# Moving the second root of a norm ahead of the residual at the seam of a two-block kernel

## The reference

```python
def first_block(...):
    ...
    h = h + rmsnorm(m @ w_out[l], norm_mix_post[l])
    u2 = rmsnorm(h, norm_mlp_pre[l])
    a = jnp.square(jax.nn.relu(u2 @ w_up[l]))
    h = h + rmsnorm(a @ w_down[l], norm_mlp_post[l])
def second_block(...):
    shift, scale, gate = adaln(c, w_ada_mix[i], b_ada_mix[i])
    h = rms_norm(x, norm_mix_w[i]) * (1.0 + scale) + shift
    proj = h @ w_in
    ...
```

## Time and profile before

| | |
|---|---|
| median of 3 runs | 1815.55 us (1814.15 to 1815.65) |
| profiled execution, its own time | 1813.71 us |
| its span | 1812.0 us |
| TensorE matmul busy | 1736.1 us, 96% |
| VectorE, ScalarE, GpSimd busy | 884.9, 689.5, 824.9 us |
| last down tile read, first product of the second block | 741.82, 770.32 us |

### The profile page before, as it was taken

The page is one execution under the profiler, slowest core; times in us unless marked ns, Lnnn a source line. Parts: engine busy times, 40 slices in busy tenths (PEclk is TensorE's granted clock), DMA queues, the critical chain, the costliest instruction groups (busy, mean ns, idle before and its releaser), DMA issues. The chain is left out here.

```text
span 1812.0 us, 22090 instructions
## 1 busy us (share of the span) xinstructions
PE 1736.1 (96%) x7978; PEld 1399.6 (77%) x7978; DVE 884.9 (49%) x1246; ACT 689.5 (38%) x934; POOL 824.9 (46%) x610
## 2 busy tenths in 40 slices
PE   7999999889999999599999999999999999999997
PEld 5777776768888888478887878777888788888886
DVE  3343356373444445469888887874515411101112
ACT  4333254422222222246547464665523323222231
POOL 4333434544464646434343434425346344664453
PEclk9999999999999999799999999999999899999998
DMA  4121112335353534223323223212222222332232
GB/s 175 70 70 69 69 70 73 113 130 183 126 199 119 196 118 158 70 78 99 128 93 116 93 93 116 93 70 71 92 93 93 93 93 93 116 139 93 93 116 93
DMA packets 30198, 193.25 MB, mean 107 GB/s; under 512 B 3360, under 2 KB 3360, under 8 KB 11328
## 3 DMA queue, kind: packets, MB, share of 16 engines
q1 hardware_dynamic: 23184, 158.89, 24.6%
q10 hardware_dynamic: 6960, 33.62, 5.5%
HBM read 190.34 MB, written 2.16 MB: 106 GB/s over the span
## 5 line engine op out<-in xcount | busy, mean ns | idle before, releaser
L405 POOL TENSOR_TENSOR w_lo<-w_raw,w_hi 128x512 fp32r<-128x512 f32 x588 | 804.6, 1400 | 960.3 <-ACT w_hi L913 960.3
L430 PE MATMUL gemm_bank<-a_hi,w_hi 128*128 128x512 f32 x1224 | 487.9, 399 | 0.3 <-ACT w_hi L913 0.3
L431 PE MATMUL gemm_bank<-a_lo,w_hi 128*128 128x512 f32 x1224 | 478.6, 391 | 0.0
L913 ACT ACTIVATE w_hi<-w_raw 128x2048 fp32r<-128x2048 f32 x147 | 280.3, 1907 | 220.5 <-PE gemm_bank L437 173.3
L437 PE MATMUL gemm_bank<-a_hi,w_lo 128*128 128x512 f32 x1224 | 308.9, 395 | 4.4 <-POOL w_lo L405 4.4
L430 PEld LDWEIGHTS gemm_bank<-a_hi,w_hi 128*128 128x128 f32 x1224 | 230.8, 189 | 55.2 <-issue 7.8
L437 PEld LDWEIGHTS gemm_bank<-a_hi,w_lo 128*128 128x128 f32 x1224 | 229.0, 189 | 56.1 <-POOL w_lo L405 6.1
L431 PEld LDWEIGHTS gemm_bank<-a_lo,w_hi 128*128 128x128 f32 x1224 | 230.8, 189 | 48.2 <-issue 1.9
L1623 DVE SCALAR_TENSOR_TENSOR aux_bank<-scratch,gcol,aux_bank 128x511 f32<-128x511 f32 (+15 forms) x240 | 165.7, 733 | 15.0 <-ACT aux_bank L1105 12.7
L468 PE MATMUL gemm_bank<-a_hi,w_hi 128*128 128x512 f32 x352 | 130.3, 415 | 25.3 <-ACT a_hi L923 17.6
L430 PE MATMUL gemm_bank<-b_hi,w_hi 128*128 128x512 f32 x368 | 148.7, 404 | 0.0
(11 more groups left out here) (274 smaller groups left out, 2072.4 us busy)
## 6 DMA issues: line engine op xcount, KB each, us to landing
w_raw<-weights_dram SPq DMA_DIRECT2D x147, 1024.0 KB, 4.7
arena<-ada_dram ACTq DMA_DIRECT2D x32, 768.0 KB, 4.3
acc<-cum_rows ACTq DMA_DIRECT2D x8, 512.0 KB, 3.8
h<-x_t_dram SPq DMA_DIRECT2D x4, 512.0 KB, 7.4
row_b<-cum_rows ACTq DMA_DIRECT2D x4, 512.0 KB, 4.8
scratch<-cum_rows ACTq DMA_DIRECT2D x4, 512.0 KB, 4.3
out_t_dram<-arena SPq DMA_DIRECT2D x8, 256.0 KB, 2.2
cols<-cols_dram SPq DMA_DIRECT2D x1, 279.0 KB, 2.8
```

What stands on the lines that cost most here:

```text
L405: ins = pool.tensor_tensor(wlo[s][:, w], raw[s][:, w], whi[s][:, w].bitcast(F32), ALU.subtract)
L430: pe.matmul(gemm_bank[bank][:, :], whi[slot][:, w], hi[:, k, :], start=(n == 0), stop=False)
L431: pe.matmul(gemm_bank[bank][:, :], whi[slot][:, w], lo[:, k, :], start=False, stop=False)
L913: act.activation(whi[panel % 2][:, :], raw[panel % 2][:, :], ACT.Copy).then_inc(w_hi_ready, 1)
```

## The change

The root of the second block's norm is no longer taken from squares of the new `h`. With r the inverse root of the MLP's norm, the sum of squares of h + r (gain y) is r squared times the sum of (gain y) squared, plus 2 r times the sum of gain y h, plus the sum of h squared. The last is kept from the earlier norm (`h_sum`); the other two are added up beside the last down tiles (`gained_sum`, `cross_sum`), on ScalarE and VectorE. TensorE sums the three behind the last tile, the last chunk apart. VectorE puts them together in five 128x4 steps (`new_sum`). The second inverse has a buffer and a bank of its own (`rinv2`, `aux[2]`). VectorE makes the added parts in three buffers, GpSimd adds them to `h`, VectorE multiplies the operand. The first product of the second block starts three tiles together (T_DT and both of panel 57), where there were two and one. The residual behind the mixer passes its product through PSUM banks instead of `tmp`. Panel 26 is rounded ahead of the MLP's relus. The small gains `gain2` are made beside chunk 6 of the last down tiles.

```diff
+cross = acc31[:, 1, :]
+cross_sum = row_b[:, 1, :]
+gained_sq = [tmp[:, 0, :], tmp[:, 1, :]]
+gained_sum = acc31[:, 0, :]
+step3 = [tmp[:, 0, :], tmp[:, 1, :], acc31[:, 0, :]]
...
+panels_of(0, P_MLP // 2 + 1)
+add_squares(pool, 1)
+panels_of(P_MLP // 2 + 1, P_DT // 2 + 1)
+for k in range(KC):
+    pool.wait_ge(post_step, KC + k + 1)
+    pool.tensor_tensor(h[:, k, :], h[:, k, :], step3[k % 3], ALU.add).then_inc(h_ready, 1)
+panels_of(P_DT // 2 + 1, P_END // 2)
...
+def sums_of_parts():
+    pe.wait_ge(sq_sum_step, 17)
+    pe.wait_ge(gained_step, KC - 2)
+    pe.wait_ge(cross_step, 2 * (KC - 2) + 1)
+    for n, of in ((0, sq_sum), (1, gained_sum), (2, cross_sum)):
+        for j in range(QT):
+            mm = pe.matmul(aux[0][:, 3 * j + n:3 * j + n + 1], of[:, j * P:(j + 1) * P], ones[:, 0:1],
+                           start=(n == 0 and j == 0), stop=False, skip_group_check=True)
+    mm.then_inc(early_sums, 1)
+def sums_of_last():
+    pe.wait_ge(cross_step, 2 * (KC - 2) + 2)
+    for j in range(QT):
+        pe.matmul(aux[0][:, 3 * j + 2:3 * j + 3], cross[:, j * P:(j + 1) * P], ones[:, 0:1],
+                  start=False, stop=False, skip_group_check=True)
+    pe.wait_ge(ysq_ready, 16)
+    for j in range(QT):
+        mm = pe.matmul(aux[0][:, 3 * j:3 * j + 2], sq[:, 1, j * P:(j + 1) * P], one_gain2[:, :],
+                       start=False, stop=(j == QT - 1), skip_group_check=True)
+    mm.then_inc(sum_done, 2)
 mlp(0, True)
 with pe.Fori(1, MLP_GROUPS) as i:
     mlp(i, False)
-sums_of_sum(17, 16)
+sums_of_parts()
+sums_of_last()
 spread(3)
-sums(2)
-spread(4)
-tile_pair([(0, P_DT, T_DT, 0, 0, wide(0)), (0, P_GRP, T_GRP, 0, 0, wide(0))], a_hi, a_lo,
-          (a_hi_ready, 3 * KC + 1), (a_lo_ready, 3 * KC + 1), True)
+pe.wait_ge(rinv_ready, 5)
+for j in range(QT):
+    mm = pe.matmul(aux[2][:, j * P:(j + 1) * P], rinv2[:, j:j + 1].to_broadcast([P, P]), ident[:, :],
+                   start=True, stop=True)
+mm.then_inc(r_ready, 1)
+def first_three():
+    three = [(P_DT, T_DT, 0), (P_GRP, T_GRP, 0), (P_GRP, T_GRP + 1, 1)]
+    for k in range(KC):
+        pe.wait_ge(a_hi_ready, 3 * KC + k + 1)
+        for panel, t, j in three:
+            w = slice((2 * k + j) * P, (2 * k + j + 1) * P)
+            if k == 0:
+                pe.wait_ge(w_hi_ready, panel + 1)
+                pe.wait_ge(bank_free[t % 4], t // 4 + 1)
+            pe.matmul(gemm_bank[t % 4][:, :], whi[panel % 2][:, w], a_hi[:, k, :], start=(k == 0), stop=False)
+            if k == 0:
+                pe.wait_ge(w_lo_ready, panel + 1)
+            pe.matmul(gemm_bank[t % 4][:, :], wlo[panel % 2][:, w], a_hi[:, k, :], start=False, stop=False)
+    for k in range(KC):
+        pe.wait_ge(a_lo_ready, 3 * KC + k + 1)
+        for panel, t, j in three:
+            w = slice((2 * k + j) * P, (2 * k + j + 1) * P)
+            mm = pe.matmul(gemm_bank[t % 4][:, :], whi[panel % 2][:, w], a_lo[:, k, :],
+                           start=False, stop=(k == KC - 1))
+            if k == KC - 1:
+                mm.then_inc(tile_done, 1)
+first_three()
...
-g(1)
...
+round_weights(0, P_MLP + 2, 0, T_MLP + 2, 0)
...
-if j % 2 == 1:
+if j % 2 == 1 and not (first and j == 1):
...
+if j < KC - 1:
+    if j >= 3:
+        act.wait_ge(gained_step, j - 2)
+    act.activation(gained_sq[j % 2] if j else gained_sum, y[:, j, :], ACT.Square,
+                   scale=col("norm_mlp_post", j)).then_inc(sq_ready, 1)
...
-roots(3, sum_done, 4)
-squares(2)
-roots(4, sum_done, 5)
+mlp(0, True, False)
+with act.Fori(1, MLP_GROUPS - 1) as i:
+    mlp(i, False, False)
+mlp(MLP_GROUPS - 1, False, True)
+act.wait_ge(sum_done, 4)
+act.activation(root[:, :], aux[0][:, 0:3 * QT].rearrange("p (j n) -> p j n", n=3)[:, :, 0], ACT.Sqrt,
+               bias=eps[:, 0:1], scale=1.0 / D).then_inc(root_ready, 1)
+act.wait_ge(new_step, 5)
+act.activation(root[:, :], new_sum[:, :], ACT.Sqrt, bias=eps[:, 0:1], scale=1.0 / D).then_inc(root_ready, 1)
...
+if n == 2:
+    dve.tensor_copy(h_sum[:, :], aux[0][:, 0:QT])
...
-    dve.scalar_tensor_tensor(tmp[:, k % 2, :], y[:, k, :], col(gain, k), aux[1][:, :],
+    dve.scalar_tensor_tensor(aux[2 + k % 2][:, :], y[:, k, :], col(gain, k), aux[1][:, :],
                              ALU.mult, ALU.mult).then_inc(post_step, 1)
 if k >= 1:
     dve.wait_ge(post_step, base + k)
-    dve.tensor_tensor(h[:, k - 1, :], h[:, k - 1, :], tmp[:, (k - 1) % 2, :], ALU.add) \
+    dve.tensor_tensor(h[:, k - 1, :], h[:, k - 1, :], aux[2 + (k - 1) % 2][:, :], ALU.add) \
...
+if last:
+    if j >= 2:
+        dve.wait_ge(cross_step, 2 * j - 1)
+    if j == KC - 1:
+        dve.wait_ge(early_sums, 1)
+    dve.scalar_tensor_tensor(cross if j else cross_sum, y[:, j, :], col("norm_mlp_post", j), h[:, j, :],
+                             ALU.mult, ALU.mult).then_inc(cross_step, 1)
 if last and j < 7:
+    if j:
+        dve.wait_ge(cross_step, 2 * j)
+        dve.tensor_tensor(cross_sum, cross_sum, cross, ALU.add).then_inc(cross_step, 1)
     dve.wait_ge(ysq_ready, 8 + j + 1)
     dve.wait_ge(sq_sum_step, 10 + j)
     dve.tensor_tensor(sq_sum, sq_sum, sq[:, j % 2, :], ALU.add).then_inc(sq_sum_step, 1)
+    if j:
+        dve.wait_ge(sq_ready, 2 * KC + j + 1)
+        if j >= 2:
+            dve.wait_ge(gained_step, j - 1)
+        dve.tensor_tensor(gained_sum, gained_sum, gained_sq[j % 2], ALU.add).then_inc(gained_step, 1)
+if last and j == KC - 2:
+    dve.wait_ge(mod_ready, MLP_GROUPS)
+    for part, name in enumerate(("norm_mix_w", "norm_ffn_w")):
+        dve.scalar_tensor_tensor(gain2[:, KC * part:KC * part + KC],
+                                 mod[:, 24 * part + KC:24 * part + 2 * KC], 1.0,
+                                 cols[:, COLS[name]:COLS[name] + KC], ALU.add, ALU.mult) \
+            .then_inc(gain2_ready, 1)
...
-residual(3, "norm_mlp_post", 8, 24)
-dve.wait_ge(mod_ready, MLP_GROUPS)
-for part, name in enumerate(("norm_mix_w", "norm_ffn_w")):
-    dve.scalar_tensor_tensor(gain2[:, KC * part:KC * part + KC], mod[:, 24 * part + KC:24 * part + 2 * KC], 1.0,
-                             cols[:, COLS[name]:COLS[name] + KC], ALU.add, ALU.mult).then_inc(gain2_ready, 1)
+def summed(n):
+    return aux[0][:, 0:3 * QT].rearrange("p (j n) -> p j n", n=3)[:, :, n]
+def added_part(k):
+    if k >= 3:
+        dve.wait_ge(h_ready, KC + k - 2)
+    dve.scalar_tensor_tensor(step3[k % 3], y[:, k, :], col("norm_mlp_post", k), aux[1][:, :],
+                             ALU.mult, ALU.mult).then_inc(post_step, 1)
+def new_operand(k):
+    dve.wait_ge(h_ready, KC + k + 1)
+    dve.scalar_tensor_tensor(a_raw[:, k, :], h[:, k, :], gain2[:, k:k + 1], aux[2][:, :],
+                             ALU.mult, ALU.mult).then_inc(pre_raw, 1)
+inverse(3)
+dve.wait_ge(rinv_ready, 4)
+dve.tensor_tensor(new_sum[:, :], summed(1), rinv[:, :], ALU.mult).then_inc(new_step, 1)
+dve.wait_ge(new_step, 1)
+dve.scalar_tensor_tensor(new_sum[:, :], summed(2), 2.0, new_sum[:, :], ALU.mult, ALU.add).then_inc(new_step, 1)
+dve.wait_ge(new_step, 2)
+dve.tensor_tensor(new_sum[:, :], new_sum[:, :], rinv[:, :], ALU.mult).then_inc(new_step, 1)
+dve.wait_ge(new_step, 3)
+dve.tensor_tensor(new_sum[:, :], new_sum[:, :], h_sum[:, :], ALU.add).then_inc(new_step, 1)
+dve.wait_ge(new_step, 4)
+dve.tensor_scalar(new_sum[:, :], new_sum[:, :], 0.0, None, ALU.max).then_inc(new_step, 1)
+dve.wait_ge(r_ready, 4)
+added_part(0)
+inverse(4)
+added_part(1)
+added_part(2)
 dve.wait_ge(gain2_ready, 2)
-dve.wait_ge(h_ready, 2 * KC)
-normed_shifted(4, 2, 3 * KC, 0)
+dve.wait_ge(r_ready, 5)
+for k in range(KC):
+    new_operand(k)
+    if k + 3 < KC:
+        added_part(k + 3)
+for k in range(KC):
+    dve.wait_ge(a_hi_ready, 3 * KC + k + 1)
+    dve.scalar_tensor_tensor(a_lo[:, k, :], a_raw[:, k, :], mod[:, k:k + 1], a_hi[:, k, :].bitcast(F32),
+                             ALU.add, ALU.subtract).then_inc(a_lo_ready, 1)
```

27 lines of the change are left out of this document (15 added, 12 removed).

## The result

The changed kernel took 1800.56 us (median of 4 runs, 1798.72 to 1800.85), the kernel before beside it 1815.6 (1814.15 to 1817.13): ratio 0.9911, 95% interval 0.9897 to 0.9925. So 15.0 us faster; the two profiled executions differ by 12.9 in their spans (1812.0 and 1799.1). The forecast was 11.2 faster, 1804.4, with a range of 1798 to 1809.5.

What follows compares the result with a forecast made beforehand. TensorE, busy 96% of 1812.0 us, was taken as the bound, so time is won where it idles or runs slowly. Head -2.7 and junction -8.5 make -11.2: 1804.4 us against the median 1815.55, range 1798 to 1809.5.

Steps and rivals of the forecast that it cites:

- The seam, to the first product: Between the blocks, last projection read to next block's first product: first product at 757.1, 13.2 earlier; gap 28.5 to 15.
- The small steps: Five 128x4 VectorE steps between the two roots, some held by GpSimd: 3.0 taken, 1.0 with none waiting, 5.0 with three.
- The outer bounds 754.4 and 759.9: Next block's first product, in the old trace's clock: 754.4 with no waits in the steps, 759.9 with all.
- GpSimd's addition: Residual add to h between the blocks: 1.53 a chunk, the median of 1.29 to 1.77 for GpSimd's two-operand steps.
- the rival of the GpSimd pace: First three tiles: GpSimd's adds take 2.3 a chunk, the operand comes 5 later, 1809 in all; chance 0.07.
- Given back: Behind the first three tiles: ScalarE's chain up to the sigmoid loses its cover; 4.7 us lost, junction -13.2 + 4.7 = -8.5.
- The head of the MLP: First block, residual through PSUM and panel 26 rounded early: stage -2.7, from -0.7 to -5.5.
- 2.0, 1.75 and 0.7: VectorE's gains in the MLP's head: residual, step no longer meeting GpSimd, waiting gone; together 4.5.
- The residual through PSUM: First block's adds to h: 0.38 less each, eight times 3.0; 2.0 taken, between 0 and 3.0.
- The rule weighed: Skill's rule: two-SBUF-input VectorE and SBUF-reading GpSimd instructions exclude each other; all SBUF-only small steps could be held, 2.0 later.
- the first rival: MLP wait really goes or small steps aren't held: clock stays up, junction starts near 755; 1800 to 1802, chance 0.17.
- the signs listed ahead: Gap of 15, small steps over 0.8, adds 1.3 to 1.8, sigmoid 5 behind tiles, panel 58 idling, `b_hi` wait 3 to 4.

Runs made afterwards that it cites:

- e4: The changed kernel without VectorE's wait for `early_sums` before the last cross product; 1799.22 us.
- e11: e8 with the results of the second to fifth of VectorE's five small steps in PSUM instead of SBUF; 1794.75 us.
- e5: The changed kernel with both edits at the MLP's head undone: residual product in SBUF, panel 26 rounded at its old place; 1809.42 us.
- a0: The changed kernel again, unedited, as the base of the follow-up set; 1801.66 us.
- e2: The changed kernel with panel 26 rounded at its old place, behind the second relu; 1802.82 us.
- e7: The changed kernel with the decay's exp moved to the program's start, so no Exp table is loaded behind the first tiles; 1800.78 us.
- e3: The changed kernel with two tiles together at the seam and the third behind them, as before the change; 1796.06 us.
- e1: The changed kernel with the first block's residual product back in an SBUF tile; 1802.66 us.
- e8: The changed kernel with two tiles at the seam, the third behind, and VectorE's wait for the early sums left out; 1794.35 us.
- e9: e8 with 1, 2 and 4 thrown-away 128x512 products in TensorE's three waits at the seam; 1793.50 us.

## Why the prediction held, point by point

**The seam, to the first product: right, 14.3 for 15.3.** The mechanism held, but the number is in part luck, since steps missed in both directions. The last chunk and the sums were let wait 1.2: the early sums follow TensorE's last product after 0.28, so nothing was late. But the eight last matmuls, put at 2.3, took 3.2, and that used the gain up: the first reciprocal ended 7.5 behind the last read, exactly as foreseen. The last product behind the `early_sums` wait was there as written (2.28 idle on VectorE, 0.93 on TensorE). The small steps were put at 3.0 between 1.0 and 5.0; they took 1.4 (745.17 to 746.59), with one held for 0.62. From the same order they took 1.0 to 2.0 in the other kernels; in e4, with two held for 1.2 each, they took 3.0, and in e11, with none held, 1.0. The 5.0 was never reached. That left 1.6 too much in the sum, of which 0.8 went to a wait that it did not have: at the low clock the first spread lasts until 747.28, and the first added part, with the second reciprocal behind it, waits for that (0.72). The outer bounds 754.4 and 759.9 are given without their full working; the small steps alone make 2.0 of it each way. GpSimd's addition was put at 1.53 a chunk, the median of the earlier trace rows, and took 1.3: those rows were taken beside VectorE steps with two SBUF operands, and here each of VectorE's reads one operand from PSUM, which is the likely reason. So the rival of the GpSimd pace did not come: nowhere did the three tiles wait, and they took the 18.3 foreseen.

**Given back: right, 4.9 for 4.7.** Between the first product and the running sums it is 4.7 too, but that exact match is luck: the same code gives 4.4 to 5.8 there, with the clock of the first products (granted from the fourth to the sixth us: 1.00 in e5 with its 35.7, 0.91 in the change, 0.72 in a0, 0.55 in e2 with its 37.0). From the end of the tiles it is 4.9 in every kernel with the three together but e7. Every link of the chain took its time (the sigmoid starts 4.9 behind the tiles), e7 removed one and the distance fell by its length, 1.5, and e3 removed all of it with the third tile behind as cover.

**The head of the MLP: direction right, -5.1 for -2.7.** The wait of the earlier trace rows did go. VectorE's eighth relu, put at 4.5 earlier, came 4.7 earlier. What failed is the step "TensorE arrives sooner than that and idles about 4 us there; the products behind it then run slow, 1.8": there is no wait ahead of the down tiles. A down tile takes the rounded chunks one after another, and its 16 products start at 415.30, before the last chunk is rounded (416.60) and without standing still. TensorE was itself held up by the low part of the next panel (2.0 at 406.32), which the prediction did not see: GpSimd begins panel 27 only at 398.33 and needs 7.9 for it. So the 1.8 taken off for slow products had no cause. Nor were the two parts to be summed: 2.0, 1.75 and 0.7 were added up as independent gains, where e1, e2 and e5 show 3.6 for either alone and 4.7 to 6.1 for both at the eighth relu. That their sum fitted is luck: in the profiled run nothing of the 2.0 was left at the first relu, and all 4.7 came behind it, where the sum had 2.45.

**The residual through PSUM: 2.0, measured 1.6 at its place against the kernel before, 2.5 against e1; what is left at the end is within the scatter.** "1.065 against 0.687" was read as the price of a second SBUF operand. It is the price of GpSimd beside two.

**The rule weighed.** All-SBUF small steps can be held and ones with a PSUM operand can't, as e4, e8 and e11 show. But a step is held only up to the end of the GpSimd instruction that it meets (1.19 at most, where one of four takes 4.92 / 4 = 1.23), and not each one meets it: in the change the two steps after the held one ran when GpSimd had ended its panel (746.18). In all eight kernels that keep this order and the `early_sums` wait, one step is held, and it ends 0.01 to 0.03 behind the panel's end; it took 0.24 to 1.15, by where in the last low part it fell. So the cost of such a step is drawn by phase, between nothing and one GpSimd instruction.

**The total** of -11.2 stands against -12.9 in the spans: the head gave 2.4 more than foreseen, the seam and the give-back together 1.0 more, and unchanged code took 1.7. Against the medians it is 3.8 short: 1800.56 lies below the forecast proper (1802 to 1806.5, chance 0.50), in the wider range and in that of the first rival (1800 to 1802, chance 0.17). And that rival is what came: the clock did not fall at the eighth relu, and the small steps were held less. Its junction near 755 came by half: counted from the last read in the old trace's time, the first product stands at 756.1, for 757.1 in the sum. Of the signs listed ahead, the gap, the sigmoid behind the tiles, TensorE's idling for panel 58 and the end of the wait at 397 came; no small step was over 0.8, and no wait of 3 to 4 stood ahead of the down tiles.

## What to carry to other kernels

When work is pulled ahead of a seam, look at what had covered the next engine's chain: a tile left behind the seam was worth more here than in it (4.9 us, and a version at 1796, with the needless wait removed too at 1794). Two repairs of one stretch need not add up; undo them apart and together before either is given a price. Before a distance from one trace is called an effect, look at how far it varies between kernels with the same code there. And read a slow instruction's rows against the other engine's before its operands are blamed.

## What was not expected

A VectorE addition of two 128x512 SBUF tiles takes 0.68 us with GpSimd idle, as quick as with a PSUM operand, and 1.0 to 1.8 beside it. The Trainium skill ("SBUF — State Buffer", section "Who interferes with whom") has this rule, that such an instruction contends only with a GpSimd one that reads SBUF, and that a one-input step in a two-port mode does too; the `TENSOR_SCALAR` of e4, held 1.19 with one SBUF input, and the same step in PSUM at 0.17 in e11 agree with it. The rule as the prediction weighed it left this exception out.

Seven products of 128x512 without use, in waits of 0.6 to 1.7 us, brought TensorE's granted clock from 0.50 to 0.97 in the stretch up to the first products (e9), and won next to nothing, since another engine's pace was the bound. And a delay of 2.5 us ahead of a tile (e1) came out as 0.8 behind it, as the earlier version ran that tile at half clock.
